# Four low-half subtractions of a Strassen-like projection move from VectorE to GpSimd

## What is computed

```
ya = (oa * jax.nn.silu(hgate)) @ w_branch_a[i]
yb = (ob * jax.nn.silu(ngate)) @ w_branch_b[i]
y = jax.nn.sigmoid(m_a) * ya + jax.nn.sigmoid(m_b) * yb
x = x + y @ w_out[i]
g = jax.nn.sigmoid(_rms(x, ple_norm[i]) @ w_ple_gate[i])
x = x + (p[i] @ w_ple[i]) * g
```

## Time and profile before

| what | value |
|---|---|
| median of three timed runs | 1796.05 us |
| time of the profiled execution | 1796.85 us |
| its span | 1795.1 us |
| PE busy | 1763.7 us (98% of the span) |
| DVE busy | 1282.5 us (71%) |
| ACT busy | 865.2 us (48%) |
| POOL busy | 197.8 us (11%) |
| the first group of the output projection | 1423.3 to about 1504.6 us from the span's start |

### The profile page before, as it was taken

The page is one execution under the profiler, slowest core; times in us unless marked ns, Lnnn a source line. Parts: engine busy times, 40 slices in busy tenths (PEclk is TensorE's granted clock), DMA queues, the critical chain, the costliest instruction groups (busy, mean ns, idle before and its releaser), DMA issues.

```text
span 1795.1 us, 23833 instructions
## 1 busy us (share of the span) xinstructions
PE 1763.7 (98%) x9241; PEld 1513.3 (84%) x9241; DVE 1282.5 (71%) x1546; ACT 865.2 (48%) x1169; POOL 197.8 (11%) x204
## 2 busy tenths in 40 slices
PE   6999999999999999999999999999999999999998
PEld 5899999888888888888888888888888877888887
DVE  6977777777687777878787878794555588874433
ACT  7444444434474747565656575655222343544221
POOL 4000000000040403031313121221000000000000
PEclk9999999999999999999999999999999999999999
DMA  7354444675723333333333333334555456542332
GB/s 225 89 141 122 117 124 144 213 246 176 200 84 109 87 112 87 100 88 106 93 106 92 95 104 94 103 105 144 164 144 150 152 195 230 184 141 94 118 118 82
DMA packets 287269, 236.81 MB, mean 132 GB/s; under 512 B 7977, under 2 KB 232264, under 8 KB 286656
## 3 DMA queue, kind: packets, MB, share of 16 engines
q1 hardware_dynamic: 284064, 225.48, 41.9%
q0 software_dynamic: 3104, 9.96, 1.7%
HBM read 215.00 MB, written 20.41 MB: 131 GB/s over the span
## 4 chain that ended last, share of the span: by engine, by line
PE 90%; DVE 5%; issue 2%; DMA 2%; ACT 1%; SPq 0%; DVEq 0%; ACTq 0%
PE mm_ps L2054 13%; PE mm_ps L2052 13%; PE mm_ps L2053 13%; PE ax_ps L2039 2%; PE ax_ps L2041 2%; PE ax_ps L2040 2%; PE ax_ps L2052 2%; PE ax_ps L2054 2%; PE ax_ps L2053 2%; PE mm_ps L2277 2%; PE mm_ps L2278 2%; PE mm_ps L2276 2%; PE mm_ps L2040 2%; PE mm_ps L2041 2%; PE mm_ps L2039 2%
## 5 line engine op out<-in xcount | busy, mean ns | idle before, releaser
L364 DVE TENSOR_TENSOR w_lo<-w_raw,w_hi 128x1024 fp32r<-128x1024 f32 x188 | 235.9, 1256 | 252.2 <-ACT w_hi L355 252.1
L2052 PE MATMUL mm_ps<-act_hl,w_hi 128*128 128x512 f32 x960 | 383.3, 399 | 0.0
L355 ACT ACTIVATE w_hi<-w_raw 128x1024 fp32r<-128x1024 f32 x188 | 198.4, 1056 | 373.0 <-PE mm_ps L2054 157.7
L2054 PE MATMUL mm_ps<-act_hl,w_lo 128*128 128x512 f32 x960 | 375.2, 391 | 0.0
L2053 PE MATMUL mm_ps<-act_hl,w_hi 128*128 128x512 f32 x960 | 374.8, 390 | 0.0
L2054 PEld LDWEIGHTS mm_ps<-act_hl,w_lo 128*128 128x128 f32 x960 | 180.3, 188 | 38.6
L2053 PEld LDWEIGHTS mm_ps<-act_hl,w_hi 128*128 128x128 f32 x960 | 180.6, 188 | 36.1
L2052 PEld LDWEIGHTS mm_ps<-act_hl,w_hi 128*128 128x128 f32 x960 | 180.6, 188 | 35.7
L1056 ACT ACTIVATE q_hi<-q_raw 128x1024 fp32r<-128x1024 f32 x84 | 87.6, 1057 | 141.7 <-DVE q_raw L1420 81.2
L1411 DVE TENSOR_TENSOR q_lo<-q_raw,q_hi 128x1024 fp32r<-128x1024 f32 x84 | 101.8, 1224 | 52.6 <-ACT q_hi L1056 52.1
L928 POOL TENSOR_TENSOR key<-key,low_h 128x512 f32<-128x512 f32 x16 | 16.8, 1051 | 804.8 <-ACT key L1163 804.8
(11 more groups left out here) (373 smaller groups left out, 4187.3 us busy)
## 6 DMA issues: line engine op xcount, KB each, us to landing
w_raw<-in_w_in SPq DMA_DIRECT2D x120, 512.0 KB, 3.8
q_raw<-in_w_in SPq DMA_DIRECT2D x56, 512.0 KB, 6.0
r_in<-in_w_in SPq DMA_DIRECT2D x56, 512.0 KB, 4.6
w_raw<-in_w_out SPq DMA_DIRECT2D x36, 512.0 KB, 5.2
w_raw<-in_w_ple_gate SPq DMA_DIRECT2D x32, 512.0 KB, 3.8
w_raw<-in_w_branch_a SPq DMA_DIRECT2D x16, 512.0 KB, 4.0
w_raw<-in_w_branch_b SPq DMA_DIRECT2D x16, 512.0 KB, 4.0
r_mid<-in_w_out SPq DMA_DIRECT2D x16, 512.0 KB, 5.6
```

The costliest lines, as they stand in the source:

```text
L355: nc.scalar.activation(w_hi[:, s, :], w_raw[:, r, :], ACT.Copy).then_inc(hi_done, 1)
L364: nc.vector.tensor_tensor(w_lo[:, s, :], w_raw[:, r, :], w_hi[:, s, :].bitcast(F32), ALU.subtract).then_inc(lo_done, 1)
L2052: MM(bank, wh, m_hi[:, k0 + k, :], start=start and k == 0, stop=False)
L2054: mm = MM(bank, wl, m_hi[:, k0 + k, :], start=False, stop=stop and k == kn - 1)
```

## The change

GpSimd makes the low halves of the four sums, one behind the other and ahead of the loads of the residual. DVE no longer makes them. On ACT the high halves of the sums stand one place earlier each, and the high half of the last tile of y one place later; on DVE the low half of that tile stands two places earlier.

```diff
@@ gpsimd
+            def sy_lo(n, done):
+                pool.wait_ge(sy_hi_done, done)
+                nc.gpsimd.tensor_tensor(sy_hl[:, n - 1, :, 1], sy_source(n), sy_hl[:, n - 1, :, 0].bitcast(F32),
+                                        ALU.subtract).then_inc(sy_lo_done, 1)
+
+            sy_lo(1, 1)
+            sy_lo(2, 2)
+            sy_lo(4, 3)
+            sy_lo(3, 4)
             pool.wait_ge(sy_lo_done, 2)
             for t in range(NT):
                 pool.wait_ge(unit_done, U_OUT + 4 + 2 * t)
@@ scalar
                     o_hi(act, g, j)
-                    if g == 0 and j in (3, 4, 6, 8):
-                        sy_hi({3: 1, 4: 2, 6: 4, 8: 3}[j])
-                    if g == 0 and j == 3:
+                    if g == 0 and j in (2, 3, 5, 7):
+                        sy_hi({2: 1, 3: 2, 5: 4, 7: 3}[j])
+                    if g == 0 and j == 4:
                         y_hi(KT - 1)
@@ vector
-            def sy_lo(n, done):
-                dve.wait_ge(sy_hi_done, done)
-                TT(sy_hl[:, n - 1, :, 1], sy_source(n), sy_hl[:, n - 1, :, 0].bitcast(F32), ALU.subtract).then_inc(sy_lo_done, 1)
-
@@ vector
                         merge_y(KT - 1)
                         y_sums(7)
-                    if g == 0 and j in (5, 7, 11, 15):
-                        sy_lo({5: 1, 7: 2, 11: 4, 15: 3}[j], {5: 1, 7: 2, 11: 3, 15: 4}[j])
-                    if g == 0 and j == 6:
+                    if g == 0 and j == 4:
                         y_lo(KT - 1)
```

## The result

| | before | after |
|---|---|---|
| median of the timed runs | 1796.18 us (1795.53 to 1797.25, 4 runs) | 1806.58 us (1805.99 to 1807.4, 4 runs) |
| profiled execution | 1796.85 us | 1807.17 us |
| its span | 1795.1 us | 1805.2 us |

The ratio of the times is 1.0056, interval 1.0044 to 1.0068: the change makes the kernel 10.4 us slower. Forecast were 1807.3 us, with a range from 1802 to 1817.

A forecast was written before the change was run, and what follows sets the result against it. PE, busy for 98% of the span, gains only where it waits for low halves DVE is late with. Holds of 4.4 us make unit 12 11.1 late, with tenths 11.3; 1796.05 + 11.3 = 1807.3 us, range 1802.0 to 1817.0.

The forecast's parts named there:

- The hold of 4.4 us: First group of the output projection: each of POOL's four subtractions blocks a DVE instruction with two SBUF operands for 4.4 us.
- The bounds of 3.4 and 6.9: Lower and upper limits, in us, for how long one POOL subtraction of 2048 elements holds DVE.
- The order on ACT alone: Sums' high halves ahead of units': unit 3 2.3 us late, unit 8 at 1447.5 if DVE isn't held.
- Units 3, 4 and 5: Their starts on PE, behind held low halves on DVE: 5.8, 8.5 and 11.9 us late.
- Units 7, 8 and 12: Their starts on PE, "14" left off: about 57.0, 59.7 to 60.0 (12 late), and 70.7 (11.1, with tenths 11.3).
- some tenths: Allowance at unit 12 for a raw tile that comes late, taking its delay from 11.1 to 11.3 us.
- Nothing gives the delay back.: Behind unit 12: the group's last stretch keeps its gaps of 2.32 us, PE is busy after, so the delay stays.
- About 2 us at most: Worth of taking four subtractions off DVE: waits before units 8 and 12 go, other gaps lie 22 us behind.
- No hold: Rival: POOL doesn't hold DVE at units 3, 4 and 5; 1 us faster, 1795.0, perhaps 2 us; chance 0.09.
- POOL slower or faster: Rivals on hold length: 5.5 us gives 1811.7, 6.9 gives 1817.4 (chance 0.15); 3.4 gives 1803.4 (chance 0.1).
- The clock: Rival: PE's clock falls in the gap before unit 3; up to +3 (1810.3); chance 0.2 of costing over 1 us.
- The 3.7 us of idling: Time PE is idle before its clock falls to the lower level, read at the end of the kernel.

The follow-up runs named there:

- the kernel with the memsets: The changed kernel with two POOL memsets in place of each subtraction, the sums' low halves not computed: 1794.29 us, ratio 0.9988.
- the kernel kept busy: The changed kernel with added matmuls into an unused tile ahead of units 3, 4, 5 and 7, so PE doesn't stand still: 1806.67 us.
- the new order alone: The changed kernel with the four subtractions back on DVE in the steps where they were before: 1797.06 us, ratio 1.0000.
- the split version: Kernel before, no POOL subtractions; ACT makes seven eighths of sums 1 and 2's high halves early, DVE's first low half at j = 3: 1792.57 us, repeated 1792.91.
- POOL only: The changed kernel with ACT's order and the place of the last tile of y as before: 1805.26 us, ratio 1.0045.
- the copies: The changed kernel with POOL copying each sum in place of subtracting, the low halves not computed: 1796.11 us, ratio 0.9997.
- one subtraction whole: The split version with sum 3's low half made on POOL in one piece: 1792.95 us; with two of the four residual loads behind it, 1792.88 us.
- four pieces: The split version with sum 3's low half on POOL in four pieces, each behind another unit of PE: 1793.67 us, ratio 0.9981.
- sixteen: The changed kernel with POOL's four subtractions cut into sixteen pieces of 512 elements: 1805.66 us, ratio 1.0049.
- the repetition: The changed kernel measured again, unaltered, beside the kernel kept busy: 1807.76 us.

## Why the prediction was right, point by point

- *The hold of 4.4 us.* Right: 4.38, 4.38, 4.41 on DVE itself. The proportionality that it was scaled by holds (1.09 at 512). The bounds of 3.4 and 6.9 weren't needed; the output in fp32r costs POOL nothing that shows (4.53 us where it didn't wait).
- *The order on ACT alone.* Right in place and size for unit 3 (2.16 us of waiting in front of it). With DVE relieved it was to put unit 8 at 1447.5; in the kernel with the memsets, where DVE is relieved and not held, unit 8 starts at 1449.17. Unit 3 takes 4.45 us there (1433.79 to 1438.24) in place of 2.72: a clock that falls after a wait this short was not in the sum. Unit 12 is then 0.4 us late, and 1.9 us come back behind it, as below.
- *Units 3, 4 and 5.* Forecast 1437.2, 1442.8 and 1449.0; measured 1436.92, 1442.44 and 1448.56. The first hold was 0.9 us shorter on DVE, since POOL had started before DVE asked, as the text had it.
- *Units 7, 8 and 12.* Unit 7 at 1456.39 was 0.6 early; unit 8 was late, 1460.84 against 1459.7 to 1460.0. In this profile unit 7 itself runs at the lower clock, 4.45 us to the next unit for 2.72. Unit 12 was then 12.1 us late where 11.1 to 11.3 were forecast, and all of that comes from unit 8, since units 8 to 12 follow each other without a wait. DVE's wait of 1.95 us for a raw tile (the row at 1462.82 above), whose buffer came free behind the held instructions, is hidden here. In the kernel kept busy, where the clock stays up, it shows: unit 10 comes 0.5 us late for it and unit 11 another 0.1. The sum had "some tenths" for the tile and nothing for the clock.
- *"Nothing gives the delay back."* Wrong. From unit 12 to unit 28 takes 45.80 us after and 47.73 before: 1.9 us come back. The step that failed is the one by which the last stretch keeps all its gaps as another's work. It does keep those before units 24, 25 and 26 (3.46, 3.38 and 3.47 us from the unit ahead after, 3.56, 3.38 and 3.47 before). The one before unit 21 goes, in the kernel before and then after:

```profile
1485.64 0.50 PE L2329 MATMUL mm_ps<-w_hi,sy_hl 128*128 128x512 f32 x1 [0.93 <-DVE w_lo L558]
```

```profile
1496.24 0.39 PE L2332 MATMUL mm_ps<-w_hi,sy_hl 128*128 128x512 f32 x1
```

  From unit 20 to unit 21 it is 3.98 us before and 2.72 after. Behind it stands a sum of weights on DVE that waits for a raw tile, first before, then after:

```profile
1483.23 1.23 DVE L1847 TENSOR_TENSOR r_mid<-r_mid,w_raw 128x1024 f32<-128x1024 f32 x1 [1.62 <-DMA w_raw<-in_w_out]
```

```profile
1493.42 1.23 DVE L1852 TENSOR_TENSOR r_mid<-r_mid,w_raw 128x1024 f32<-128x1024 f32 x1 [0.90 <-DMA w_raw<-in_w_out]
```

  It starts 1.6 us behind unit 20 before, and 0.1 ahead of it after. The wait is there in each kernel in which DVE makes sum 3's low half at j = 15 (before, the new order alone, the split version: 3.6 to 4.0 us from unit 20 to 21), and absent in the ones with that work elsewhere or left out (2.72 each: after, POOL only, the memsets, the copies, one subtraction whole). The two versions in pieces are exceptions. With four pieces (4.29 us) POOL's turns, 1459 to 1469, fall between units 12 and 16, where DVE made the sum before. With sixteen (3.09) they end at 1464.65, ahead of unit 11; there DVE comes late for another reason, a wait of 1.80 us for a raw tile at 1478.56. The link read from the traces is a raw buffer that DVE frees late: the load into `r_mid` two ahead of the awaited one is issued 1.7 us before unit 18 starts in the kernel before, 2.8 us before it after, and the awaited one lands 6.8 us behind its issue before, 5.0 after. It was not tested by itself.
- The two errors, +0.8 at unit 12 and -1.9 behind it, partly cancel: 11.3 in the sum met 10.3 in the profiled executions. That much of the closeness is luck.
- *"About 2 us at most"* for the relief of DVE fails by the same step: with the memsets, where DVE is relieved and ACT has the new order, 2.7 us are won, and 1.9 us of the delay at unit 12 come back behind it. The gap before unit 21 begins 16 us behind the last of the four subtractions, not 22.
- *The rivals.* No hold: refuted by four held instructions; made real with memsets it is 1794.3. POOL slower or faster: no. The clock: it fell where the rival said, at unit 3, hidden behind the wait of unit 4, and once more at unit 7 (in the repetition at unit 5), where it said units 5 and 6; its price stayed within about 1 us, below the 3 us of the bound. The 3.7 us of idling that it worked from did not carry over: the clock was at 0.50 well within the gap before unit 3, and fell behind waits of 2.07 and 2.16 us as well. The loads of `x2a` stayed hidden: the last POOL subtraction ends at 1454.1, and the first sum with `x2a` runs at 1474.25.

## What to carry to other kernels

In these runs, work moved from VectorE to GpSimd that reads SBUF did not run beside VectorE's instructions with two SBUF operands: it was queued with them, and it took twice the time (4.4 us for 2.28) on the very engine that was to be relieved. Before moving work, look in the trace for any place where both engines compute and compare the same form alone and beside the other. What helped was to use idle time of the engines already at work: part of the high halves made while ACT waited, and DVE's first low half made while DVE waited, together 4 us.

## What the runs showed of the hardware that was not expected

- GpSimd reading one SBUF operand holds VectorE as well, for the rest of its instruction (0.83 us in the rows above); only writing (memsets, 1.8 us each at 128 x 2048, VectorE at 1.23 beside them) doesn't.
- GpSimd's copy of 128 x 2048 took 1.88 us, its subtraction 4.53, where neither waited for VectorE.
- Turns don't always alternate. The Trainium skill ("SBUF — State Buffer", Who interferes with whom) says that the second to start is blocked for the whole of the first; the trace agrees for each single hold, but GpSimd, having asked at 1453.11, let five more instructions of VectorE with two SBUF operands start and pass until 1459.9.
- The granted clock fell after a wait of only 2.16 us in the kernel with the new order alone, whereas the waits of up to 1.53 us before left it at 1.00. Two stretches of that kernel, the second beginning a microsecond behind the start of unit 3:

```profile
1430.00:1434.70 4.70, 2.54 (x11) 1.73 (x10) 1.23 (x1) 4.70 (x4) 0.00 (x0) 0.93 0.77 272
1434.70:1438.20 3.50, 3.50 (x11) 2.81 (x10) 3.14 (x4) 3.50 (x4) 0.00 (x0) 0.61 0.47 146
```

- The length of the wait alone doesn't decide it. In the two profiles of the kernel after the wait before unit 5 is 3.10 us in both; in the first the clock stays at 1.00 behind it, in the repetition it is at 0.50:

```profile
1445.50:1452.00 6.50, 3.44 (x15) 2.84 (x16) 6.50 (x4) 2.85 (x2) 4.83 (x2) 1.00 0.28 83
```

```profile
1448.50:1454.50 6.00, 5.46 (x13) 4.29 (x14) 6.00 (x3) 0.39 (x1) 5.53 (x2) 0.50 0.30 90
```
